# A second pair of spare-weight buffers in two expert stages, and another order in three of a kernel's product pairs

## The chip, the cores and the metric

The kernel runs on one core of one Trainium2 chip. The metric is device microseconds of one execution, as a median of several runs. All data is float32.

## What is computed

The reference is two networks one after the other, on 512 tokens of width 1024. The first has two layers. Each adds a mixer (pooling with chunked attention in layer 0, a Mamba-2 mixer in layer 1) and a hierarchical mixture of experts:

```python
g_val, g_idx = lax.top_k(g_prob, 1)                  # one of 4 groups
e_val, e_idx = lax.top_k(jax.nn.softmax(e_logits), 2) # two of its 8 experts
combine = jnp.sum(one_hot(expert_id, 32) * weights[..., None], axis=1)
hid = silu(einsum('td,edf->tef', t, w1)) * einsum('td,edf->tef', t, w3)   # f = 128
y = einsum('tef,efd->td', hid * combine[:, :, None], w2)
```

The second network has two layers too, on the 512 tokens and 256 tokens of context. Of the layer's wide input projection, `hx @ w_in`, come a bidirectional retention with per-head decay, a short convolution, a conformer convolution and a windowed attention; their four outputs are gated and merged, and `merged @ w_out` is added to the tokens:

```python
merged = sum(sigmoid(g) * (br @ w_branch[i]) for i, (g, br) in enumerate(zip(gates, (r, s, f, a))))
return merged @ w_out
```

In layer 0 the context is carried along; in layer 1 only its keys and values are needed.

## The kernel before, in words

Each engine has a program of its own, written out by hand in one order. `Count` (line 81) keeps the semaphore counts: a step of an engine is named (`pe.step`, `ve.step`), and another engine waits for the name (`pe.at`). What stands behind a waiting instruction on its engine waits too. Stages follow one another: mixer A, experts of layer 0, the Mamba-2 mixer, experts of layer 1, then the two layers of the second network.

**The expert stage** (`moe`, lines 789 to 900 on TensorE, 1335 on SyncE, 1557 on ScalarE, 2295 on VectorE, 2897 on POOL). A step handles two halves of 64 lanes, each with an expert of its own. There are 16 static steps for the 32 experts in order and 8 spare steps for experts that more than 64 tokens chose. `ORDER` (line 39) is two static steps, then a spare one, and so on: 24 steps. For step i TensorE does `rows_T` (transposes of the gathered token rows, two steps ahead), `up` (32 products 128x256, one step ahead), `hid_T` and `down` (8 products 128x512). `down` ends with the mark `step_done`.

Weights of a static expert, 1536 KB, are loaded by SyncE's queue into one of `HELD` = 7 buffers (line 370 ff.): five in `arena`, one in two ring slots and `square`, one in `hT`. Expert e waits for `step_done` of static step (e - HELD) // 2 (line 1338). Weights of spare experts come by indirect gathers from POOL (`spare`, line 2910): 128 rows of 12 KB per half into `spare_w`, two buffers in ring slots 0 to 5. Spare block j waits for the spare step before it. A block that no tokens need has row numbers out of bounds, and its gather moves no weights. POOL's queue holds, in this order: three row gathers (`fetch`), `spare(0)`, two more `fetch`, and then per step i one `fetch(i+5)`, which waits for the transposes of step i+2, the scatter of the output rows, which waits for VectorE's copy, and after a spare step the next `spare`. The work arrays of the router, `route_c` to `r4`, lie in `arena` between the row buffers and the static ones.

**Product pairs** (`pair`, line 671, on TensorE). Two blocks of 128 output columns of the second network, a and b, are computed together from half-sums of weights and of inputs, with seven products in place of eight (P1, P2, P6, P5, P7, P3 and one more); each is 4 x 2 instructions. VectorE makes the weight sums S1 to S4 (`w_sums`, line 1959, and `w_sum_4`), the input sums T1 to T4, and the sums of results C11, C22, C12 (`combine`, line 1981). ScalarE copies three partial results out of the banks (`copies`, line 1720): `copy_1` after P1, `copy_2` after P6, `copy_3` after P5 and C11. P6 waits for `copy_1`, S2 and T2; P7 for `copy_2`, S3 and T3; P3 for `copy_3` and S4; the last for C22 and T4. A pair takes 28 x 2 instructions.

Two places have no earlier pair to hide these steps. The first input pair follows the attention: VectorE does T1, T2, the weight sums, T4, T3, the gate multiplies of four chunks and a memset that marks `att_done` (lines 2666 to 2684). ScalarE does `ret_decay(0)`, which waits for `att_done`, `ret_strip(0)` and then `copies` (lines 1845 to 1847); these tables hold the powers of the decay and are first used in `ret_weights(0)`, after the second pair. The first output pair (`ready == "m"`) follows the merging: P1 waits for merged rows 0 to 3, P2 for rows 4 to 7 (lines 690 to 698).

## Time and profile before

| what | value |
|---|---|
| median of 3 runs | 3615.08 us (3606.56 to 3618.36) |
| the profiled execution's own time | 3612.57 us |
| its span, first to last instruction | 3610.8 us |
| TensorE busy | 3339.2 us (92%) |
| VectorE busy | 1730.4 us (48%) |
| ScalarE busy | 877.2 us (24%) |
| POOL busy | 128.5 us (4%) |
| mean granted TensorE clock | 0.967 of full |
| DMA | 393.88 MB, mean 109 GB/s |

Spans of the trace are read in microseconds from the first instruction. A granted clock of 1.00 is the upper of TensorE's two levels, 2.4 GHz, and 0.50 the lower, 1.2 GHz. "Idle before" is the time an engine stood before a group of instructions, and the arrow names what ended it. The expert stages lie at about 350 to 560 us and 1195 to 1400 us, the second network from about 1415 us on.

### The profile page before, as it was taken

What the parts mean: (1) busy time and instruction counts of PE and PEld (TensorE: products, weight loads), DVE (VectorE), ACT (ScalarE), POOL (GpSimd) and SP (SyncE); (2) the same over time, 40 slices, a digit from 0 to 9 for tenths busy, and PEclk for the clock granted to TensorE, in tenths of its full rate; (3) what the DMA queues carried; (4) which work ended last, traced back from release to release, by engine and by line L of the source; (5) the groups of instructions that cost most, each with busy time, mean ns of one, the idle gap of its engine ahead of it and who ended that gap; (6) DMA issues with size and microseconds to landing.
All of it is one profiled execution on the core that took longest, in us unless ns stands there. A gap on an engine that the chain in (4) does not pass through costs nothing.

```text
span 3610.8 us, 34772 instructions
## 1 busy us (share of the span) xinstructions
PE 3339.2 (92%) x12856; PEld 1965.0 (54%) x12856; DVE 1730.4 (48%) x3258; ACT 877.2 (24%) x1773; POOL 128.5 (4%) x132
## 2 busy tenths in 40 slices
PE   7987987999999797998899999999989889999998
PEld 3443553444444554555455555555544556778886
DVE  1153224555542324868533454444458853454554
ACT  2041222222331122025232121111121523222222
POOL 0000330000000230000000000000000000000000
PEclk9998998999999898999999999999999999999998
DMA  7625764767423783100111212222212011222331
GB/s 251 209 77 201 298 242 135 217 205 220 117 61 135 253 327 114 42 29 13 45 47 35 58 41 58 58 60 57 65 55 70 18 57 47 59 70 82 88 88 59
DMA packets 416917, 393.88 MB, mean 109 GB/s; under 512 B 27856, under 2 KB 353616, under 8 KB 409072
## 3 DMA queue, kind: packets, MB, share of 16 engines
q1 hardware_dynamic: 383200, 348.01, 30.8%
q10 hardware_dynamic: 15120, 23.68, 2.1%
q0 software_dynamic: 18432, 19.98, 1.7%
q8 instruction: 106, 1.74, 0.2%
q14 instruction: 59, 0.48, 0.0%
HBM read 440.78 MB, written 31.52 MB: 131 GB/s over the span
## 4 chain that ended last, share of the span: by engine, by line
PE 78%; DVE 7%; DMA 4%; ACT 4%; issue 2%; POOL 0%; ACTq 0%; DVEq 0%; POOLq 0%
PE psum L679 37%; PE psum L664 16%; PE psum L868 4%; PE psum L1059 3%; DVE arena L1944 2%; DMA ring<-in_moe_w,spare_u 2%; PE psum L1150 2%; PE psum L887 2%; ACT arena L1419 2%; PE psum L1198 2%; DMA ring<-in_w_branch 1%; PE psum L735 1%; PE psum L1218 1%; PE psum L1230 1%; PE psum L764 1%
## 5 line engine op out<-in xcount | busy, mean ns | idle before, releaser
L679 PE MATMUL psum<-arena,ring 128*128 128x384 f32 (+1 forms) x2592 | 750.6, 440 | 37.0 <-ACT part_sum L1419 23.4
L664 PE MATMUL psum<-hT,ring 128*128 128x512 f32 (+1 forms) x1728 | 706.0, 567 | 17.7 <-DVE hT L1937 15.4
L679 PEld LDWEIGHTS psum<-arena,ring 128*128 128x128 f32 x2592 | 494.3, 191 | 264.0 <-ACT part_sum L1419 25.8
L679 PE MATMUL psum<-hT,ring 128*128 128x384 f32 (+1 forms) x2176 | 621.8, 439 | 0.0
L664 PEld LDWEIGHTS psum<-hT,ring 128*128 128x128 f32 x1728 | 327.7, 192 | 390.0 <-issue 377.2
L679 PEld LDWEIGHTS psum<-hT,ring 128*128 128x128 f32 x2176 | 413.3, 190 | 188.7 <-issue 6.9
L1419 ACT ACTIVATE arena<-psum 128x512 f32<-128x512 f32 (+5 forms) x501 | 210.2, 466 | 571.3 <-PE psum L664 285.4
L1941 DVE TENSOR_TENSOR ring<-ring 128x512 f32<-128x512 f32 (+1 forms) x336 | 215.7, 661 | 269.9 <-PE psum L679 267.3
L1419 ACT ACTIVATE part_sum<-psum 128x384 f32<-128x384 f32 (+1 forms) x324 | 142.7, 440 | 817.7 <-PE psum L679 813.8
L1411 ACT ACTIVATE arena<-psum,cols 128x256 f32<-128x256 f32 (+3 forms) x280 | 133.1, 494 | 683.3 <-PE psum L868 227.7
L1941 DVE TENSOR_TENSOR psum<-psum,part_sum 128x384 f32<-128x384 f32 (+1 forms) x244 | 120.0, 497 | 288.8 <-PE psum L679 280.0
L1941 DVE TENSOR_TENSOR arena<-arena 128x512 f32<-128x512 f32 (+13 forms) x252 | 186.3, 753 | 107.4 <-ACT arena L1419 57.9
L1944 DVE SCALAR_TENSOR_TENSOR arena<-arena,psum 128x128 f32<-128x128 f32 (+3 forms) x284 | 115.2, 430 | 252.9 <-ACT arena L1411 225.3
L1944 DVE SCALAR_TENSOR_TENSOR arena<-arena,vec 128x783 f32<-128x783 f32 (+1 forms) x256 | 228.7, 893 | 9.1
L1411 ACT ACTIVATE arena<-arena,cols 128x512 f32<-128x512 f32 (+8 forms) x199 | 158.1, 828 | 63.5 <-DVE cols L2684 20.3
L868 PE MATMUL psum<-ring,arena 128*64 128x256 f32 x640 | 100.3, 429 | 27.2 <-DMA ring<-in_moe_w,spare_u 27.2
L1941 DVE TENSOR_TENSOR arena<-psum,part_sum 128x384 f32<-128x384 f32 (+1 forms) x80 | 40.8, 510 | 170.6 <-PE psum L679 170.4
L679 PE MATMUL psum<-arena,square 128*128 128x384 f32 (+1 forms) x384 | 113.9, 432 | 3.7 <-DVE arena L1941 3.7
L1059 PE MATMUL psum<-arena,ring 128*128 128x512 f32 x256 | 110.7, 593 | 0.0
L868 PE MATMUL psum<-arena 128*64 128x256 f32 x768 | 102.5, 383 | 0.0
L868 PEld LDWEIGHTS psum<-ring,arena 128*64 128x64 f32 x640 | 65.4, 155 | 63.2 <-DMA ring<-in_moe_w,spare_u 37.4
L1944 DVE SCALAR_TENSOR_TENSOR xT<-psum,cols,xT 128x512 f32<-128x512 f32 (+1 forms) x64 | 37.6, 611 | 125.7 <-PE psum L1059 65.1
(233 smaller groups left out, 2995.0 us busy)
## 6 DMA issues: line engine op xcount, KB each, us to landing
ring<-in_w_in SPq DMA_DIRECT2D x172, 512.0 KB, 4.1
arena<-in_moe_w SPq DMA_DIRECT2D x48, 1536.0 KB
ring<-in_ada_w SPq DMA_DIRECT2D x96, 512.0 KB, 5.5
ring<-in_ssm_w_in SPq DMA_DIRECT2D x48, 512.0 KB, 6.5
ring<-in_w_mod SPq DMA_DIRECT2D x48, 512.0 KB, 4.8
ring<-in_w_branch SPq DMA_DIRECT2D x64, 256.0 KB, 3.1
hT<-in_moe_w SPq DMA_DIRECT2D x8, 1536.0 KB
ring<-in_mix_w_in SPq DMA_DIRECT2D x16, 512.0 KB, 7.8
```

The source lines that it names most:

```text
L664: mm = nc.tensor.matmul(b[:, 0:n], ws[k // 8][0][:, k % 8, :], rhs(k)[:, o:o + n], start=(k == 0), stop=(k == nk - 1))
L679: mm = nc.tensor.matmul(flat(bank_, nb), lhs[:, k, :], rhs(k), start=(start and k == 0), stop=(k == kd_ - 1), skip_group_check=True)
L735: mm = nc.tensor.matmul(b[32 * j:32 * j + 32, :], csilu[:, int(q >= 6), k, :], w, start=(k == 0), stop=(k == KD - 1), skip_group_check=True)
L868: mm = nc.tensor.matmul(b[LANES * h:LANES * h + LANES, 0:2 * P], rowsT[:, i % 2, k, LANES * h:LANES * h + LANES], step_weights(s, h, 2 * P ...
L887: mm = nc.tensor.matmul(b[LANES * h:LANES * h + LANES, :], hidT[:, i % 2, LANES * h:LANES * h + LANES], step_weights(s, h, w0, S), start=T ...
L1059: mm = nc.tensor.matmul(b, ws[k // 8][0][:, k % 8, :], yT[:, k, :], start=(k == 0), stop=(k == 15))
L1150: mm = nc.tensor.matmul(b[:, 0:w], z_w[c][0][:, k, :], hT[:, k, o:o + w], start=(k == 0), stop=(k == KD - 1))
L1198: mm = nc.tensor.matmul(b[0:64, :], v_tok[:, t, 64 * j:64 * j + 64], pT2[:, kb, :], start=(i == 0), stop=(i == len(tiles) - 1))
L1411: return nc.scalar.activation(out_, in_, f, bias=bias, scale=scale, **kw)
L1419: return nc.scalar.activation(out_, in_, ACT.Copy)
L1941: return v.tensor_tensor(out_, in0, in1, op)
L1944: return v.scalar_tensor_tensor(out_, in0, s, in1, op0, op1)
```

## The change

The static experts get six buffers in place of seven, and the spare experts four in place of two: the new pair is the area of the router's work arrays and the freed static buffer. Spare block j then waits for the spare step two before it. Block 1's gather goes into the POOL queue behind `fetch(4)`, behind a wait for the last token transposes and for `w_slot`, and in layer 0 behind two memsets that clear the new buffers. `w_slot` gets a tile of its own. Experts 4 and 5 take the buffers, and the waits, that experts 5 and 6 had. In the first input pair of each layer, VectorE makes the weight sums ahead of the input sums and T3 ahead of T4, and ScalarE's `copies` and VectorE's `combine` of this pair go ahead of the decay tables. In the first output pair of each layer P5 goes between P1 and P2; `w_sums` waits for P6 too.

```diff
-HELD = 7
+HELD = 6
...
+        w_slot = sb("w_slot", [P, STEPS])[:, :]
...
-        held = [in_thirds(arena[:, held_at + EW * i:held_at + EW * (i + 1)]) for i in (3, 4, 0, 1, 2)]
+        held = [in_thirds(arena[:, held_at + EW * i:held_at + EW * (i + 1)]) for i in (3, 4, 0, 1)]
...
-        spare_w = [ring[:, 3 * i:3 * i + 3, :, :].rearrange("p a k n -> p (a k n)") for i in range(2)]
+        assert routed_at + EW <= held_at
+        spare_tiles = [ring[:, 0:3].rearrange("p a k n -> p (a k n)"), ring[:, 3:6].rearrange("p a k n -> p (a k n)"),
+                       arena[:, routed_at:routed_at + EW], arena[:, held_at + 2 * EW:held_at + 3 * EW]]
+        spare_w = [in_thirds(t) for t in spare_tiles]
...
                 product(x, wa[:, 0:kd_, :], low(0), True, ("P1", a))
-                w, w_full = job(*a, "0")
                 if ready == "m":
+                    z, z_full = job(*a, "1")
+                    eng.wait_ge(vector_done, pe.at(("S1", a)))
+                    eng.wait_ge(vector_done, pe.at(("T1", ready, a[1])))
+                    product(z, s(0), total(0), True, ("P5", a))
                     for c in range(4, 8):
                         eng.wait_ge(vector_done, pe.at(("mrg", a[1], c)))
+                w, w_full = job(*a, "0")
                 product(w, wa[:, kd_:2 * kd_, :], high(0), True, ("P2", a))
...
                 product(x, s(1), total(1), False, ("P6", a))
-                z, z_full = job(*a, "1")
-                eng.wait_ge(vector_done, pe.at(("S1", a)))
-                product(z, s(0), total(0), True, ("P5", a))
+                if ready != "m":
+                    z, z_full = job(*a, "1")
+                    eng.wait_ge(vector_done, pe.at(("S1", a)))
+                    product(z, s(0), total(0), True, ("P5", a))
...
-                            eng.wait_ge(spare_landed[h], pe.at(("spare", l, s - STATIC, h)))
+                            eng.wait_ge(spare_landed[2 * (s % 2) + h], pe.at(("spare", l, s - STATIC, h)))
...
-                    elif e == 5:
+                    elif e == 4:
                         eng.wait_ge(tensor_done, sp.at(("full",) + jobname("route", l)))
-                    elif e == 6:
+                    elif e == 5:
                         eng.wait_ge(tensor_done, sp.at(("full",) + jobname("h_tok", l, 3, 1)))
...
                     todo = pairs(l)
+                    copies(*todo[0])
                     ret_decay(0)
                     ret_strip(0)
-                    copies(*todo[0])
...
                 if last:
                     eng.wait_ge(tensor_done, ve.at(("P5", last)))
+                    eng.wait_ge(tensor_done, ve.at(("P6", last)))
...
+                    if l == 0:
+                        eng.wait_ge(tensor_done, ve.at(("full",) + jobname("att_z", l, 0, "x0")))
+                    w_sums(*todo[0])
+                    w_sum_4(*todo[0])
                     eng.wait_ge(tensor_done, ve.at(("full",) + jobname("pt2", l, 7, x_tiles(l)[-1], "x")))
...
                     tt(rows_of(1), hi1, rows_of(0), ALU.subtract).then_inc(vector_done, ve.step(("T2", "h", l)))
-                    if l == 0:
-                        eng.wait_ge(tensor_done, ve.at(("full",) + jobname("att_z", l, 0, "x0")))
-                    w_sums(*todo[0])
-                    w_sum_4(*todo[0])
+                    tt(lo1, hi1, lo1, ALU.subtract).then_inc(vector_done, ve.step(("T3", "h", l)))
                     eng.wait_ge(vector_done, ve.own())
                     tt(rows_of(2), hi0, rows_of(1), ALU.subtract).then_inc(vector_done, ve.step(("T4", "h", l)))
-                    tt(lo1, hi1, lo1, ALU.subtract).then_inc(vector_done, ve.step(("T3", "h", l)))
...
+                    combine(*todo[0])
                     decay(0)
-                    combine(*todo[0])
...
                 def spare(j):
 
-                    if j:
-                        eng.wait_ge(tensor_done, po.at(("step_done", l, STATIC + j - 1)))
+                    if j >= 2:
+                        eng.wait_ge(tensor_done, po.at(("step_done", l, STATIC + j - 2)))
+                    elif j:
+                        eng.wait_ge(tensor_done, po.at(("full",) + jobname("h_tok", l, 3, 1)))
+                        eng.wait_ge(vector_done, po.at(("w_slot", l)))
+                        if l == 0:
+                            g.memset(spare_tiles[2], 0.0).then_inc(gpsimd_done, po.step())
+                            g.memset(spare_tiles[3], 0.0).then_inc(gpsimd_done, po.step("spare_clear"))
+                            eng.wait_ge(gpsimd_done, po.at("spare_clear"))
...
                     for h in range(2):
-                        eng.indirect_dma_start(spare_w[h], None, a[f"moe_w_{l}"].rearrange("e p n -> (e p) n"),
+                        q = 2 * (j % 2) + h
+                        eng.indirect_dma_start(spare_tiles[q], None, a[f"moe_w_{l}"].rearrange("e p n -> (e p) n"),
...
                 fetch(DEEP)
                 fetch(DEEP + 1)
+                spare(1)
...
-                    if s >= STATIC and s + 1 < STEPS:
-                        spare(s + 1 - STATIC)
+                    if s >= STATIC and s + 2 < STEPS:
+                        spare(s + 2 - STATIC)
```

## Rows read from the trace of the kernel before

**Rows 1.** The page, costliest groups of instructions.

```profile
L1419 ACT ACTIVATE part_sum<-psum 128x384 f32<-128x384 f32 (+1 forms) x324 | 142.7, 440 | 817.7 <-PE psum L679 813.8
...
L868 PE MATMUL psum<-ring,arena 128*64 128x256 f32 x640 | 100.3, 429 | 27.2 <-DMA ring<-in_moe_w,spare_u 27.2
```

**Rows 2.** Chain of waits, layer 1's experts: start us, us, what.

```profile
1194.75 3.58 PE psum L843 x16
...
1212.77 3.45 PE psum L868 x32
...
1229.32 7.17 DMA ring<-in_moe_w,spare_u
1236.58 5.36 PE psum L868 x32
...
1361.09 3.45 PE psum L868 x32
```

**Rows 3.** Chain of waits, layer 0's experts.

```profile
372.83 3.45 PE psum L868 x32
...
518.82 3.45 PE psum L868 x32
...
525.27 3.45 PE psum L868 x32
```

**Rows 4.** Timeline of POOL: start, us, engine, line, what, idle before.

```profile
362.23 0.98 POOL L2906 DMA_INDIRECT arena<-h_dram,pair_u  x1 [0.61 <-PE psum L853]
371.23 0.98 POOL L2906 DMA_INDIRECT arena<-h_dram,pair_u  x1 [8.02 <-PE psum L853]
...
1227.99 1.02 POOL L2917 DMA_INDIRECT ring<-in_moe_w,spare_u  x1 [0.30 <-issue]
```

**Rows 5.** Windows: us, busy (count) of five engines, PEclk, DMA share, GB/s.

```profile
395.41:510.60 115.19, 104.08 (x735) 61.14 (x736) 30.28 (x60) 24.40 (x60) 39.65 (x40) 0.94 0.87 322
442.86:465.69 22.83, 19.58 (x148) 11.56 (x148) 6.06 (x12) 4.86 (x12) 9.04 (x9) 1.00 0.98 359
1213.00:1229.00 16.00, 16.00 (x128) 9.37 (x124) 4.55 (x9) 3.24 (x8) 6.03 (x6) 1.00 0.95 374
1281.90:1302.50 20.60, 19.58 (x147) 11.59 (x147) 6.07 (x13) 4.86 (x12) 8.03 (x8) 1.00 0.93 353
```

**Rows 6.** Timeline of layer 0's first input pair.

```profile
1730.50 1.75 DVE L1941 TENSOR_TENSOR arena<-hT 128x1536 f32<-128x1536 f32 x1
...
1732.82 5.43 PE L679 MATMUL psum<-hT,ring 128*128 128x384 f32 x16
...
1733.96 2.61 DVE L1941 TENSOR_TENSOR ring<-ring 128x512 f32<-128x512 f32 x4
...
1744.43 0.06 DVE L2684 MEMSET cols<- 128x1 f32 x1
1744.58 3.86 ACT L1411 ACTIVATE arena<-arena,cols 128x512 f32<-128x512 f32 x5 [10.88 <-DVE cols L2684]
...
1748.87 7.36 PE L679 MATMUL psum<-arena,ring 128*128 128x384 f32 x16 [10.62 <-ACT part_sum L1419]
1748.94 0.56 DVE L1941 TENSOR_TENSOR arena<-psum,part_sum 128x384 f32<-128x384 f32 x1 [0.18 <-ACT part_sum L1419]
```

**Rows 7.** Timeline of layer 1's first input pair.

```profile
2908.52 3.72 PE L679 MATMUL psum<-hT,ring 128*128 128x256 f32 x16
...
2918.72 0.06 DVE L2684 MEMSET cols<- 128x1 f32 x1
...
2923.06 5.65 PE L679 MATMUL psum<-arena,ring 128*128 128x256 f32 x16 [10.82 <-ACT part_sum L1419]
```

**Rows 8.** Timeline of the first output pair, layer 0 and layer 1.

```profile
2595.99 16.39 PE L679 MATMUL psum<-arena,ring 128*128 128x384 f32 x45 [5.23 <-DVE arena L1941]
...
3537.88 15.30 PE L679 MATMUL psum<-arena,ring 128*128 128x256 f32 x62 [3.98 <-DVE arena L1941]
```

**Rows 9.** Groups of instructions by line and shape, VectorE's memset.

```profile
L2767 DVE MEMSET arena<- 128x1570 f32 x2 | 2.7, 1367 | 0.6 <-issue 0.6
```

More of the change, by code:

```diff
@@ L244, in program @@
         expert_landed = [sems(f"expert_{i}") for i in range(HELD)]
-        spare_landed = [sems(f"spare_{i}") for i in range(2)]
+        spare_landed = [sems(f"spare_{i}") for i in range(4)]
         y_back_landed = [sems(f"y_back_{i}") for i in range(4)]
@@ L350, in program @@
         logitT = scan_one
+        routed_at = mE.at
         route_c = mE.take(ROUTE_W)
@@ L359, in program @@
         spare_t = mE.take(2, 2 * SPARE)
-        w_slot = mE.take(STEPS)
         e_col = mE.take(16)
@@ L383, in step_thirds @@
         def step_thirds(s, h):
-            return held[(2 * s + h) % HELD] if s < STATIC else in_thirds(spare_w[h])
+            return held[(2 * s + h) % HELD] if s < STATIC else spare_w[2 * (s % 2) + h]
         def step_weights(s, h, at, n):
@@ L1343, in moe @@
                         eng.wait_ge(tensor_done, sp.at(("full",) + jobname("out" + "AM"[l], 0, "x")))
+                    elif e == 4:
+                        eng.wait_ge(tensor_done, sp.at(("full",) + jobname("route", l)))
                     elif e == 5:
-                        eng.wait_ge(tensor_done, sp.at(("full",) + jobname("route", l)))
-                    elif e == 6:
                         eng.wait_ge(tensor_done, sp.at(("full",) + jobname("h_tok", l, 3, 1)))
@@ L1349, in moe @@
                     to = held[e % HELD]
-                    if e % HELD < 5:
-                        i = (3, 4, 0, 1, 2)[e % HELD]
+                    if e % HELD < 4:
+                        i = (3, 4, 0, 1)[e % HELD]
                         eng.dma_start(arena[:, held_at + EW * i:held_at + EW * (i + 1)], w).then_inc(expert_landed[e % HELD], sp.landing(f"expert_{e % HELD}", ("expert", l, e)))
-                    elif e % HELD == 5:
-                        eng.dma_start(ring[:, RING2:RING2 + 2].rearrange("p s k n -> p (s k n)"), w[:, 0:2 * D]).then_inc(expert_landed[5], sp.landing("expert_5", None))
-                        eng.dma_start(to[2], w[:, 2 * D:3 * D]).then_inc(expert_landed[5], sp.landing("expert_5", ("expert", l, e)))
+                    elif e % HELD == 4:
+                        eng.dma_start(ring[:, RING2:RING2 + 2].rearrange("p s k n -> p (s k n)"), w[:, 0:2 * D]).then_inc(expert_landed[4], sp.landing("expert_4", None))
+                        eng.dma_start(to[2], w[:, 2 * D:3 * D]).then_inc(expert_landed[4], sp.landing("expert_4", ("expert", l, e)))
                     else:
-                        eng.dma_start(hT[:, 0:6, 0:S], w.rearrange("p (k n) -> p k n", n=S)).then_inc(expert_landed[6], sp.landing("expert_6", ("expert", l, e)))
+                        eng.dma_start(hT[:, 0:6, 0:S], w.rearrange("p (k n) -> p k n", n=S)).then_inc(expert_landed[5], sp.landing("expert_5", ("expert", l, e)))
                 eng.wait_ge(tensor_done, sp.at(("step_done", l, ORDER[-1])))
@@ L2292, in route @@
                 b, free = full("w_slots", l)
-                ts(w_slot, b[:, 0:STEPS], 0.5).then_inc(vector_done, ve.step(free))
+                ts(w_slot, b[:, 0:STEPS], 0.5).then_inc(vector_done, ve.step([free, ("w_slot", l)]))
             def moe(l):
@@ L2916, in spare @@
                     for h in range(2):
-                        eng.indirect_dma_start(spare_w[h], None, a[f"moe_w_{l}"].rearrange("e p n -> (e p) n"),
+                        q = 2 * (j % 2) + h
+                        eng.indirect_dma_start(spare_tiles[q], None, a[f"moe_w_{l}"].rearrange("e p n -> (e p) n"),
                                                bass.IndirectOffsetOnAxis(ap=spare_u[:, 2 * j + h:2 * j + h + 1], axis=0),
                                                bounds_check=row_limit,
-                                               oob_is_err=False).then_inc(spare_landed[h], po.landing(f"spare_{h}", ("spare", l, j, h)))
+                                               oob_is_err=False).then_inc(spare_landed[q], po.landing(f"spare_{q}", ("spare", l, j, h)))
                 eng.wait_ge(h_rows_stored, 64 * (l + 1))
```

## The prediction, made before the changed kernel was run

> **What bounds the kernel now.** I read the page first. TensorE is busy for 92% of the span, so time can only come from stretches in which it stands still or runs slowly. The costliest groups show one such wait in the expert stage: the up products of the spare steps stood 27.2 us for the gather into `ring` [rows 1]. The chain of waits of the two expert stages says how it comes about. A step without a wait starts 6.45 us after the one before (518.82 to 525.27), but every third step (a spare one) hangs on down product, copy, scatter issue, gather issue and the gather's landing, 7.17 us after its issue began at 1229.32 [rows 2, 3]. The POOL timeline has the first of the two gathers leave at 1227.99, after the scatter of the same step, and its product is due one step later [rows 4]. After the stand the up product runs at the lower clock level: 5.36 us in place of 3.45 [rows 2]. The windows of the DMA engines come next, since the weights flow through the same stage: their share is 0.87 over five groups, up to 0.98 in one [rows 5]. Then I looked at the places of the other two edits: TensorE stands 10.62 us (layer 0) and 10.82 us (layer 1) in the first input pair, for the copy that ScalarE makes only behind the decay tables, which wait for the memset that closes VectorE's gate multiplies [rows 6, 7], and 5.23 and 3.98 us in the first output pair, for the merged rows [rows 8].
>
> **Spare buffers, what goes.** With two pairs of buffers, the gather of spare block j waits for spare step j-2 instead of j-1. It keeps its place on the POOL queue, so a gather leaves as late in its group as before, but its product is due four steps later (25.8 us) and not one (6.45 us). Against 7 us of landing that is ample. Between the starts of up products 2 and 22 lie 20 steps: 372.83 to 525.27 is 152.4 us in layer 0, 1212.77 to 1361.09 is 148.3 in layer 1; at 6.45 each they would take 129.0. Upper bound of the gain: 23.4 + 19.3 = 42.7 us. It has the slow products in it.
>
> **Spare buffers, what comes.** The price is one static buffer: six, not seven. Expert e then waits for static step (e-6)//2, so both experts of static step s are released by step s-3. For even s that is three steps (19.35 us) ahead of use, for odd s two (12.9 us); before, only the second expert of an odd step had so little, the first had more. What the queue must carry per group of three steps is 322 GB/s x 115.19 us / 5 = 7.42 MB [rows 5], of it 6.3 MB static weights. In 19.35 us that asks for 383 GB/s. The trace's fullest stretches: 374 GB/s at a share of 0.95 over 16 us, 353 at 0.93 over 20.6, 359 at 0.98 over a whole group. Divided by their shares that is 394, 380 and 366 GB/s, so a group needs 18.8 to 20.3 us of full queue: as much as TensorE takes. At 394 a pair of experts with its share of rows (3.7 MB) lands 9.4 us after release, 3.5 us before an odd step wants it; at 366 the lag grows by 1 us a group and uses this up after three or four of the 6.7 groups, then 1 us a group is lost. Bounds per layer: 0 and 4 us of standing, to which slow products may add 2. I take the middle, 2.5. Net: 42.7 - 5 = 37.7 us.
>
> By the Trainium skill (HBM Reference, Specifications) a core has effectively about 358 GB/s, while one streaming alone measures about 425. The stretch with 374 GB/s lies above the first figure, so I don't take it for a cap; by it a group would last 20.7 us, by the second 17.5 and nothing would be lost.
>
> **Clearing the new buffers** (layer 0 alone): two POOL memsets of 128x3072. The trace has no POOL memset of size; VectorE's nearest is 1367 ns for 1570 elements [rows 9], which scales to 2.7 us each. Below nothing it can't go, as it stands on POOL's own queue; above, I allow three times that, 16 us for both. POOL stood 8.02 us between fetch 4 and fetch 5 there [rows 4]. The two new gathers (1.3 us each with issue gap) and the scatter and fetch behind the memsets move by what exceeds this, at most 11 us. Fetch 5 left at 371.2 and is transposed after up product 4, near 389, of which 7 us are landing; spare block 1 is due at up product 5, by 392, 28 us after POOL was free. I cost the clears at nothing; they count only above 17 us. The new waits for the transposes and the slot weights are met by then: the product for the latter ended at 1198.3 in layer 1, before fetch 3 [rows 2]. The buffer numbers of experts 4 and 5 shift with their waits; they are used 40 us later: nothing.
>
> **First input pair, layer 0** [rows 6]. ScalarE's first copies no longer stand behind the tables (3.86 us of exponentials, after the memset at 1744.43). VectorE makes the weight sums first (2.61 us), then T1, T2 (1.76 each): from 1730.6, T2 is there at 1736.7, before P1 and P2 end at 1738.2 (1732.82 + 5.43). So the third product starts at 1738.2 and not at 1748.87. T3 is ready at 1738.4, T4 at 1740.2. The third copy needs C11, which VectorE makes after the four gate multiplies and the memset (1744.5 + 0.56), the copy ends at 1745.7 and its product is due at 1746.3. Gain: 10.6 us, and the two products after the stand take 5.43 instead of 7.36: 1.9. Together 12.6. The tables, which with their last steps fill the 4.4 us from 1744.43 to 1748.87, now lie beside pair 1, seven products or 18.8 us on TensorE; their first user follows that pair: nothing.
>
> **Layer 1** [rows 7]: products are 1.73 us, so C11 is the next late one. P6 starts at 2912.4 instead of 2923.06 (10.7) and P6, P5 lose their slowness (5.65 to 3.7: 2.0). P5 and P7 end at 2917.5, but VectorE's memset is at 2918.72, C11 at 2919.2, the copy (0.4) at 2919.7: a stand of 2.3 us, with perhaps 1 us of lower clock behind it. Net 9.5 (bounds 8.5 and 10.5). P5 now waits for nothing there.
>
> **First output pair** [rows 8]. P5 moves into the stand for the merged rows 4 to 7: its needs (S1, T1) are met 1.7 us into it. The stand shrinks by one product (2.7 and 1.7 us). But P5 also covered the copy between P6 and P7: 0.44 us on average [rows 1] and hand-overs, some 0.7 and 0.6 now bare. Net 2.0 + 1.1 = 3.1. The added wait of VectorE for P6 is met where P5 still comes last, and here P6 is two products earlier than P5 was.
>
> **Sum.** 37.7 + 12.6 + 9.5 + 3.1 = 62.9 us off the profiled execution's 3612.57 (span 3610.8, 1.8 around it) gives 3549.7. The median of the runs, 3615.08, is 2.5 above that execution, so 3552 for the median.
>
> **Rivals.**
> A, the forecast: 3552, between 3545 (no stand on static weights) and 3560. Chance 0.66.
> B, the static weights become the bound: the queue sustains only 353 GB/s, the raw rate of its 20.6 us row. A group lasts 21.0 us, 1.65 too long, 10.7 us in 6.5 groups, less 3 of slack: 8 per layer, and up to 7 more if each stand slows an up product by 1.9. Time 3563 to 3577, 3570 taken. For it: the share 0.98 at 359 GB/s. Against: 374 over 16 us. Chance 0.23. The skill's 358 GB/s would land here.
> C, the edit of the input pair gives its gain back: the tables, now in pair 1, hold ScalarE when pair 1 wants its first copy. Layer 1 has little room: they follow pair 0's sums there, from about 2922, and pair 1 wants its first copy from 2925.3. Were they not hidden at all, they would cost 4.4 us a layer and 1.9 of slow products: 12.6 us together, 3565. Chance 0.06.
> D, slower than before: odd static steps. Should a pair of experts take L from release to landing, because rows, scatters and gathers share its engines, the step stands L - 12.9 and runs 1.9 slow. The expert stages lose against before from L = 14.3 on; to eat the other 25 us too, L must pass 16.1. At 17.5 a group takes 25.9 us against 22.7: 45 us in 14 groups, less 25, gives 3635. The trace speaks against it: two pairs went through in 16 us together. Chance 0.03.
> E, the change doesn't remove the wait: the gathers would have to land 25 us after issue; or the clears take over 17 us, once, and spare block 1 waits for the excess: 3555 to 3570. Chance 0.02.
>
> **How the numbers follow.** The range runs from 3542 (both bounds of A and the 2.5 between median and profiled run) to 3578 (B, C). About one in ten lies outside; each side's ends come from the bounds above. A measurement here can tell about 0.3%, 11 us, from no change. Only D is slower, and only a mixture of B, C and E near 3604 would be the same: faster 0.96, same 0.02, slower 0.02.
>
> **What the changed profile would show.** Right: no idle before up products for a gather into the spare buffers; steps of 6.45 us for most of both expert stages, clock 1.0; DMA share above 0.95; third product of the first input pair at once behind the second in layer 0, and a stand of about 2 us for a copy in layer 1; 2.5 us in place of 5.23 before the second product of the first output pair. Wrong: TensorE idle ended by a load from `in_moe_w` into the static buffers (B, or D if over 3 us each), up products of 5.36 us in many steps, a new wait of pair 1 for ScalarE's copy (C), POOL memsets of over 8 us (E).

## The result, and the profile after

The changed kernel takes 3562.2 us (median, 3559.4 to 3563.9), the kernel before 3612.6 in the same comparison: a ratio of 0.986 with a 95% interval of 0.9841 to 0.9879, 1.4% faster. The profiled executions have spans of 3610.8 and 3557.5 us, 53.3 apart, where the forecast's sum took off 62.9. By the medians it is 50.4 us, since the profiled execution was the fastest of its four.

The page of the changed kernel, whose parts 1 and 5 answer to [rows 1]:

```profile
span 3557.5 us, 34884 instructions
...
PE 3329.7 (94%) x12856; PEld 1959.4 (55%) x12856; DVE 1729.6 (49%) x3258; ACT 877.3 (25%) x1773; POOL 134.3 (4%) x134
...
L1428 ACT ACTIVATE part_sum<-psum 128x384 f32<-128x384 f32 (+1 forms) x324 | 142.5, 440 | 819.9 <-PE psum L683 807.8
```

Lines have moved by 4 to 19 (L679 is now L683, L868 is L877, L1419 is L1428). The group of up products that stood 27.2 us for spare gathers has no such wait left. TensorE does the same 12856 products in 9.5 us less busy time, and its mean granted clock is 0.971 where it was 0.967. Of POOL's 5.8 us more, the two clears are 5.3.

The chain of waits over layer 0's experts in the changed kernel (start us, us, what) answers to [rows 3]:

```profile
374.56 3.45 PE psum L877 x32
...
406.83 0.40 issue
407.23 3.67 PE psum L877 x32
...
446.18 1.34 issue
447.51 3.67 PE psum L877 x32
...
467.09 2.11 issue
469.21 3.67 PE psum L877 x32
...
508.15 3.45 PE psum L877 x32
```

From up product 2 to up product 22 it is now 508.15 - 374.56 = 133.6 us, where [rows 3] have 152.4. At 6.45 a step it would be 129.0 (the shortest measured below is 129.06). What is left are stands ahead of up products 7, 13 and 16, which the chain puts under "issue": it names nothing that ended them. In the program these products wait for the loads of their static experts from SyncE's queue, whose landings the view does not show; that the loads are what they stand for is what the experiments on bytes and release below show. All three are odd static steps (s = 5, 9, 11), those whose two experts are released only two steps ahead. Up products 4, 10, 19 and 22 have their experts released as late and don't stand.

The same view of layer 1, for [rows 2]:

```profile
1194.46 3.45 PE psum L877 x32
...
1226.73 2.56 issue
1229.29 5.26 PE psum L877 x32
...
1289.23 0.37 issue
1289.60 3.67 PE psum L877 x32
...
1328.54 3.45 PE psum L877 x32
```

Here it is 134.1 us where it was 148.3, with a stand of 2.56 us ahead of up product 7 that is followed by a product at the lower clock, 5.26 us for 3.45, and one of 0.37 ahead of up product 16. Up product 7 is the second of the odd static steps to use a buffer again.

Windows of the changed kernel in layer 0's expert stage (columns as in [rows 5]):

```profile
393.93:407.23 13.30, 12.90 (x99) 7.25 (x95) 4.39 (x9) 3.24 (x8) 4.05 (x4) 1.00 0.98 359
...
393.00:396.00 3.00, 3.00 (x28) 1.71 (x26) 1.38 (x2) 0.00 (x0) 1.24 (x2) 1.00 0.71 199
...
402.00:405.00 3.00, 3.00 (x29) 2.02 (x27) 0.64 (x2) 0.97 (x3) 0.42 (x1) 1.00 1.07 418
...
374.56:501.69 127.13, 123.28 (x934) 72.41 (x931) 38.33 (x76) 31.07 (x76) 49.51 (x49) 1.00 0.96 367
...
381.02:400.38 19.36, 19.36 (x149) 11.25 (x147) 6.05 (x12) 4.86 (x12) 8.07 (x8) 1.00 0.96 374
420.35:439.72 19.37, 19.37 (x150) 11.34 (x147) 6.05 (x12) 4.96 (x12) 8.09 (x8) 1.00 1.01 390
```

The share over the stage has risen from 0.87 to 0.96. A whole group of three steps moves at 390 GB/s in one place. But at 393 to 396 us the queue holds too little, 199 GB/s, because the next pair of experts is released only at 393.9, when down product 3 ends. Up product 7 gets its weights at 407.23, 13.3 us later, where they are due after 12.9. In these 13.3 us the engines moved 359 GB/s, or 4.8 MB, where the forecast counted 3.7 MB for this pair and its rows: the pair after it is issued 6.5 us into them. SyncE's timeline has the issues:

```profile
394.20 0.33 SPq L1363 DMA_DIRECT2D ring<-in_moe_w  x1
...
395.05 0.56 SPq L1366 DMA_DIRECT2D hT<-in_moe_w  x1
400.42 0.81 SPq L1361 DMA_DIRECT2D arena<-in_moe_w  x2
```

At the other stands the time from the end of the releasing down product to the up product is 14.2 and 15.0 us (up products 13 and 16 of layer 0), 15.5 and 13.3 (7 and 16 of layer 1).

The start of POOL's program, for [rows 4]:

```profile
364.71 2.67 POOL L2928 MEMSET arena<- 128x3072 f32 x1
367.31 2.67 POOL L2929 MEMSET arena<- 128x3072 f32 x1
370.25 1.00 POOL L2935 DMA_INDIRECT arena<-in_moe_w,spare_u  x1 [0.27 <-POOL arena L2929]
...
372.97 0.98 POOL L2916 DMA_INDIRECT arena<-h_dram,pair_u  x1 [0.43 <-issue]
```

The clears and the two new gathers fill the 8.02 us in which POOL stood before. Fetch 5 leaves at 372.97, 1.7 us later than before, and by 1.7 us the whole stage starts later in this execution (up product 2 at 374.56, before at 372.83).

TensorE's timeline at the first input pairs, layer 0 and layer 1, for [rows 6, 7]:

```profile
1699.04 5.43 PE L683 MATMUL psum<-hT,ring 128*128 128x384 f32 x16
...
1704.30 5.32 PE L683 MATMUL psum<-arena,ring 128*128 128x384 f32 x16
...
2862.94 3.72 PE L683 MATMUL psum<-hT,ring 128*128 128x256 f32 x16
2866.80 3.69 PE L683 MATMUL psum<-arena,ring 128*128 128x256 f32 x16
2870.33 1.89 PE L683 MATMUL psum<-hT,ring 128*128 128x256 f32 x8
2874.17 3.63 PE L683 MATMUL psum<-hT,ring 128*128 128x256 f32 x8 [1.95 <-ACT part_sum L1428]
2877.59 1.99 PE L683 MATMUL psum<-arena,ring 128*128 128x256 f32 x8
```

Layer 0 has no stand at all. Layer 1 has one of 1.95 us for the copy behind C11, and then eight products that take 3.63 us where eight at the upper clock take 1.89.

The same view at the first output pairs, for [rows 8]:

```profile
2549.55 7.09 PE L683 MATMUL psum<-arena,ring 128*128 128x384 f32 x16 [2.80 <-DVE arena L1950]
...
2557.26 3.14 PE L683 MATMUL psum<-arena,ring 128*128 128x384 f32 x9 [0.63 <-ACT part_sum L1428]
...
3485.24 4.08 PE L683 MATMUL psum<-arena,ring 128*128 128x256 f32 x10 [2.36 <-DVE arena L1950]
```

The stands of 5.23 and 3.98 us are 2.80 and 2.36, and the copy between P6 and P7 lies bare for 0.63 us.

**Where the 53.3 us come from.** I follow the same instruction in both traces and note by how much it is earlier. Each part's gain is its length before less its length after. Four product pairs have a new order, one input and one output pair in each layer:

| part | before, us | after, us | gain | forecast |
|---|---|---|---|---|
| layer 0, up product 2 to 22 | 152.4 | 133.6 | 18.9 | 20.9 |
| layer 1, up product 2 to 22 | 148.3 | 134.1 | 14.2 | 16.8 |
| first two pairs, layer 0 (P1 to the end of the second) | 49.2 | 36.4 | 12.8 | 12.6 |
| first two pairs, layer 1 | 43.4 | 34.7 | 8.7 | 9.5 |
| output pair, layer 0 (P1's block to the first token update) | 25.2 | 23.7 | 1.5 | 2.0 |
| output pair, layer 1 | 18.3 | 17.4 | 0.9 | 1.1 |
| everything else | | | -3.7 | 0 |

The last row lies at places that no edit touches. Of the 1.7 us by which up product 2 of layer 0 starts later, 1.5 are there at 328 us, ahead of the first clear and gather of the change. Later there are places where the clock falls in one execution and not in the other: a window of the changed kernel around one pair in layer 1 shows it.

```profile
3191.00:3201.00 10.00, 7.88 (x30) 6.30 (x28) 7.43 (x20) 2.60 (x7) 0.00 (x0) 0.83 0.18 52
```

The kernel before has a granted clock of 1.00 in the stretch that answers to it (3245 to 3255), and 1.7 us of the lead go there.

### The profile page after: what moved, and what is told of

It reads as the page before. It is cut to its first block, busy times and chain, and to the rows that moved or that the text cites. A ratio compares the mean times of both kernels' runs of the same rounds, so it can differ in the third digit from the quotient of the medians.

```text
span 3557.5 us, 34884 instructions
## 1 busy us (share of the span) xinstructions
PE 3329.7 (94%) x12856; PEld 1959.4 (55%) x12856; DVE 1729.6 (49%) x3258; ACT 877.3 (25%) x1773; POOL 134.3 (4%) x134
## 4 chain that ended last, share of the span: by engine, by line
PE 81%; DVE 6%; ACT 4%; DMA 2%; issue 2%; ACTq 0%; POOL 0%; DVEq 0%; POOLq 0%
PE psum L683 37%; PE psum L668 17%; PE psum L877 5%; PE psum L1068 3%; PE psum L896 2%; DVE arena L1953 2%; PE psum L1159 2%; ACT arena L1428 2%; PE psum L1207 2%; PE psum L862 1%; DMA ring<-in_w_branch 1%; PE psum L744 1%; PE psum L1227 1%; PE psum L1239 1%; PE psum L773 1%
## 5 line engine op out<-in xcount | busy, mean ns | idle before, releaser
L683 PE MATMUL psum<-arena,ring 128*128 128x384 f32 (+1 forms) x2592 | 747.7, 439 | 12.9 <-DVE arena L1950 5.2
L683 PE MATMUL psum<-hT,ring 128*128 128x384 f32 (+1 forms) x2176 | 623.7, 440 | 2.0 <-ACT part_sum L1428 2.0
L683 PEld LDWEIGHTS psum<-arena,ring 128*128 128x128 f32 x2592 | 492.7, 191 | 238.8 <-DVE psum L1950 11.5
L683 PEld LDWEIGHTS psum<-hT,ring 128*128 128x128 f32 x2176 | 414.1, 190 | 191.5 <-issue 6.9
L1428 ACT ACTIVATE arena<-psum 128x512 f32<-128x512 f32 (+5 forms) x501 | 210.4, 466 | 573.7 <-PE psum L668 289.0
L1428 ACT ACTIVATE part_sum<-psum 128x384 f32<-128x384 f32 (+1 forms) x324 | 142.5, 440 | 819.9 <-PE psum L683 807.8
L1953 DVE SCALAR_TENSOR_TENSOR arena<-arena,psum 128x384 f32<-128x384 f32 (+3 forms) x236 | 98.4, 447 | 222.6 <-ACT arena L1420 180.5
L683 PE MATMUL psum<-arena,square 128*128 128x384 f32 (+1 forms) x384 | 115.0, 435 | 3.8 <-DVE arena L1950 3.8
L877 PE MATMUL psum<-arena 128*64 128x256 f32 x960 | 110.0, 383 | 1.3 <-issue 1.3
L877 PEld LDWEIGHTS psum<-arena 128*64 128x64 f32 x960 | 70.0, 139 | 48.0 <-issue 18.1
L2327 DVE COPY arena<-psum 128x512 f32<-128x512 f32 x96 | 66.4, 691 | 57.2 <-PE psum L896 52.0
```

The costliest lines, as they stand in the source:

```text
L683: mm = nc.tensor.matmul(flat(bank_, nb), lhs[:, k, :], rhs(k), start=(start and k == 0), stop=(k == kd_ - 1), skip_group_check=True)
L877: mm = nc.tensor.matmul(b[LANES * h:LANES * h + LANES, 0:2 * P], rowsT[:, i % 2, k, LANES * h:LANES * h + LANES], step_weights(s, h, 2 * P ...
L1428: return nc.scalar.activation(out_, in_, ACT.Copy)
L1953: return v.scalar_tensor_tensor(out_, in0, s, in1, op0, op1)
L2327: v.tensor_copy(y_rows[:, i % DEEP, n * S:(n + 1) * S], b).then_inc(vector_done, ve.step([free, ("y_rows", l, i)]))
```

## The experiments

Three questions: what each part of the change is worth alone; why odd static steps still stand; and whether the layer 1 input pair's remainder can be had. In the second, the theory was that the release of a buffer comes too late for a queue that is nearly full. Rivals were a queue that cannot carry the bytes at all, and small packets of the spare gathers that slow the loads.

**Parts alone.** First the spare buffers without the other product orders (the hunks of the input and output pairs undone):

> The changed kernel with both pair edits undone, so the spare buffers alone. Theory 1 (the parts are independent, and the trace's landmarks give each its size): the expert stages keep their 133.6 and 134.1 us between up products 2 and 22, the pairs go back to their stands of 10.6 and 10.8 us: about 22 us over the changed kernel, 3584, or 29 below the kernel before. By the sum of the prediction it would be 38 below (3575). Rival: the parts overlap (an earlier expert stage lets the pairs start at another clock level or with other weights in the ring), then this run lies more than 4 us from 3584.

Measured: 3579.1 us, ratio 0.9917 (0.99 to 0.9934). The stages take 132.9 and 135.3 us, with stands at the same odd steps. The median is 4.9 us from the expected 3584, by the letter the rival's side, but 31.6 under the kernel before of its own comparison, where 29 were expected, and the landmarks of the trace are those of the theory. The input pairs have their old stands, as its timeline of TensorE shows:

```profile
1698.36 5.43 PE L683 MATMUL psum<-hT,ring 128*128 128x384 f32 x16
1714.41 2.29 PE L683 MATMUL psum<-arena,ring 128*128 128x384 f32 x3 [10.62 <-ACT part_sum L1423]
```

Then the reverse, the kernel before with only the pairs' new orders:

> The kernel before with the pair edits alone (seven static buffers, one pair of spare buffers). Theory 1: 22 us below the kernel before (12.8 and 7.2 in the input pairs, 1.5 and 0.9 in the output pairs), 3590; the expert stages unchanged, 152 and 148 us between up products 2 and 22. Prediction's sum: 25 below. Rival: less than 15 below, because part of what the changed kernel shows there is a matter of when it arrives.

Measured: 3596.4 us, ratio 0.9956 (0.9938 to 0.9973), 14.3 us under the kernel before of the same comparison. In the trace the first two pairs take 36.4 us in layer 0 and 34.7 in layer 1, as in the changed kernel. The two parts are 31.6 and 14.3 us by medians, together 45.9 of about 50: they add, within what these intervals can tell. By the median the pairs gave less than the 24 us that the table above has for them, and less than the 15 that the rival named. Both expert stages are as before (150.3 and 148.1), but the stage of layer 0 starts at 381.4 us instead of 372.8 in the profiled execution, the slowest of the four. This is jitter ahead of every edit: TensorE stood 3.25 us for a load of modulation weights there and not 1.70, and ran more of the following products at the lower clock. With these 8.6 us added to the 13.0 between the two spans, the trace speaks for the theory. The medians alone don't settle it.

**Price of the static buffer.** Six static buffers as in the changed kernel, but one spare pair as before (spare block j waits for the spare step before it; no clears; old pair orders):

```diff
-            return held[(2 * s + h) % HELD] if s < STATIC else spare_w[2 * (s % 2) + h]
+            return held[(2 * s + h) % HELD] if s < STATIC else spare_w[h]
```

> The kernel before with six static buffers in place of seven and still one pair of spare buffers: the price of the buffer by itself, with the wait for the spare gathers in place. Theory 2 (the queue is what static weights wait for, and it is not full while the spare gathers hold the stage at 22 to 23 us a group): no stand on static weights, 3613 within 4. Rival (it is the late release that makes odd static steps wait, whatever the load): odd static steps stand here too, 2 us or more a layer, 3617 or more.

Measured: 3603.1 us, ratio 0.9981 (0.9963 to 1.0), lower than both expectations. Giving the buffer away cost nothing by itself; the stages were even shorter, 147.8 and 143.6 us, and the waits for spare gathers fell from 27.2 to 23.7 us. No stand for a static load is seen, but for one of 0.2 us. So the price of the buffer only shows once the spare gathers no longer hold the steps back. That the gathers landed a little earlier fits loads that are released later and leave the queue to them, but no run settles this.

**Which step stands.** The spare step goes between the two static steps of a group, so that odd static steps come last:

```diff
-ORDER = [s for j in range(SPARE) for s in (2 * j, 2 * j + 1, STATIC + j)]
+ORDER = [s for j in range(SPARE) for s in ((2 * j, STATIC + j, 2 * j + 1) if j else (0, 1, STATIC))]
```

> The changed kernel with the spare step of groups 1 to 7 in the middle of its group instead of at its end, so that the last step is a static one and the first released experts are wanted three steps later instead of two. Theory 2 (backlog of a full queue that grows over the stage): the stage gets one step more of slack, the stands of 4.6 and 5.1 us a layer shrink to under 1.5 each, about 3555. Rival (each pair of experts that has only 12.9 us from release to use stands, backlog or not): one such window remains in each group, so the stands stay at 4 to 5 us a layer, 3562.

Measured: 3559.1 us, ratio 0.9856 (0.9839 to 0.9873). Layer 1 has no stand and takes 129.06 us; layer 0 takes 132.9, with stands in other places. Its chain of waits:

```profile
442.02 2.54 issue
444.57 3.67 PE psum L877 x32
...
502.87 0.81 issue
503.68 3.67 PE psum L877 x32
```

The stands move with the order, and 5.7 of the 9.5 us that both stages lost go: a short distance from release to use is part of their cause. The median lies between the two expectations and can't be told from the changed kernel's.

It is not all of it. Both stands that are left are ahead of static steps 8 and 14. Of the five steps that have two steps from release to use in this order (6, 8, 10, 12, 14), these are the two whose experts go to the buffers made of `ring` with `square` and of `hT`. Of the late released steps in the changed kernel's order, up products 7 and 16 have their experts there, and both stand in every stage of the six traces with its static loads and order (the changed kernel, parts alone, no empty gathers, C11 first, sums back, outputs back). Only up product 13 of layer 0, whose experts go to `arena`, stands by more than 0.3 us besides. So which buffer is loaded counts too. No run gave these steps other buffers, and why their loads land later stays open.

**Small packets.** With these inputs the spare gathers after the first block have all their row numbers out of bounds and move no weights. Here they are not issued:

```diff
+                        if j:
+                            continue
```

> The changed kernel without the gathers of spare blocks 1 to 7, which are empty for this input (each is 2 x 128 rows out of bounds); the gather of block 0 stays. Leaves out the loading of weights for those blocks. Theory 2 (bytes fill the queue): the small packets are a minor part, the stands at odd static steps shrink by a third at most, 3558 to 3562. Rival (the small packets of empty gathers are what delays the static weights): the stands vanish, 129.5 us between up products 2 and 22 in each layer, 3553.

Measured: 3565.8 us, ratio 0.9872 (0.9854 to 0.989), stages of 131.8 and 135.2 with stands at up products 7, 13 and 16 of layer 0 and 7 and 16 of layer 1 as before. The median lies above both expectations, the stages together are 0.7 us shorter. The rival of the small packets falls.

**Bytes.** Static experts from the seventh on load only the first two thirds of their weights, and their down products use what the buffer held:

> The changed kernel with experts 6 to 31 loading only their first two thirds (w1 and w3); the down products use what w2 part the buffer held. Leaves out a third of the static bytes, with the same releases. Theory 2: no stands at static steps, 129.1 us between up products 2 and 22, 3552. Rival (time from release to landing has a fixed part that a 12.9 us window misses at times): stands of 2 us or more stay in each layer, above 3556.

Measured: 3553.2 us, ratio 0.9841 (0.9823 to 0.9858), and not one stand in either stage. Its window over layer 0's stage:

```profile
374.96:504.03 129.07, 129.07 (x982) 75.02 (x980) 40.31 (x81) 32.40 (x80) 50.51 (x50) 1.00 0.75 268
```

The stands are the static loads' in the queue. This doesn't yet tell too many bytes from too late a release.

**Release.** All bytes again, but earlier. A buffer's first two thirds hold the up weights, which are free when the up product ends, one step before `step_done`:

```diff
+                for s in range(3, STATIC):
+                    eng.wait_ge(tensor_done, sp.at(("full",) + jobname("up", l, ORDER.index(s - 3))))
+                    for h in range(2):
+                        load(2 * s + h, 0, 2 * D)
+                    eng.wait_ge(tensor_done, sp.at(("step_done", l, s - 3)))
+                    for h in range(2):
+                        load(2 * s + h, 2 * D, 3 * D)
```

> The changed kernel with each static expert loaded in two parts: the first two thirds as soon as the up product that used the buffer is done (one step and the length of a down product earlier than now), the last third at step_done as now. Same bytes. Theory 2: the queue never runs dry, so a group takes the queue's own 18.8 to 19.6 us, 0 to 2 us of stands a layer, 3553 to 3557. Rival a (the mean rate of the queue is at its cap already, 367 GB/s over the stage): stands stay at 4 to 5 us, 3562. Rival b (more and smaller transfers cost more than they give): over 3563.

Measured: 3554.3 us, ratio 0.9846 (0.9828 to 0.9863), with no stand in either stage. Its windows:

```profile
372.61:501.67 129.06, 129.06 (x982) 74.97 (x980) 40.28 (x81) 32.41 (x80) 50.48 (x50) 1.00 0.95 359
...
381.00:400.00 19.00, 19.00 (x147) 11.03 (x145) 6.05 (x12) 4.86 (x12) 7.71 (x9) 1.00 1.02 391
...
420.00:440.00 20.00, 20.00 (x157) 11.67 (x155) 6.05 (x12) 4.86 (x12) 8.08 (x8) 1.00 1.02 398
```

TensorE is busy for all of the 129.06 us. The queue carries 391 to 398 GB/s where it is kept full. The bytes and the buffers are the same as in the changed kernel, so its stands are not the limit of what the queue can carry: an earlier release takes them away, those of `ring`, `square` and `hT` too. The loads also come in smaller pieces here, and no run has the pieces without the earlier release. The median is 7.9 us under the changed kernel's, but the intervals of the two ratios overlap; the stands' going is read from the trace.

Does the earlier release help the kernel before as well? Seven static buffers, one spare pair, released in two pieces:

> The kernel before, with nothing but the split release of its seven static buffers; one pair of spare buffers stays. Theory (the stands of the kernel before are those of a gather that is issued only when its one buffer comes free, whatever the static experts' loads do): the waits for the spare gathers stay, up 2 to up 22 takes 148 to 153 us in both layers, 3612. Rival (the gathers are late because they share the queue with static loads released in a lump, so that an earlier and smoother release helps them): 140 us or less, 3590 or less. A third (loads released earlier stand ahead of the gathers in the queue and make them later): over 155 us, 3620.

Measured: 3611.3 us, ratio 0.9993 (0.9982 to 1.0004), stages of 146.2 and 150.1 us. Its waits of TensorE (us in total, times, longest):

```profile
PE psum L868 <- DMA ring<-in_moe_w,spare_u: 27.7, 10, 7.2
```

The wait is that of [rows 1], 27.2 us there. The stands of the kernel before don't go with an earlier release of the static buffers; with the second spare pair they do. In this kernel the split is worth nothing that can be told.

**Layer 1's input pair.** VectorE makes C11 ahead of the gate multiplies, through the `mid` of `combine`:

```diff
-                    combine(*todo[0])
+                    combine(*todo[0], mid=att_gates)
```

> The changed kernel with C11 of the first input pair ahead of VectorE's gate multiplies and the memset instead of behind them; the decay tables stay behind the memset. Theory 3 (in layer 1 the third product waits for copy_3, which waits for C11, which waits for the gate multiplies; stand 1.95 us and some 1.6 us of lower clock after it): layer 1's input pair gains 3 to 4 us, layer 0's nothing, 3558 to 3559. Rival (weight sums and C22, now behind the multiplies, take the place of C11 as what is late): the stand moves to the last product, gain under 1 us or a loss of up to 3.

Measured: 3557.9 us, ratio 0.9856 (0.9838 to 0.9874). Its timeline of TensorE:

```profile
2868.44 3.69 PE L683 MATMUL psum<-arena,ring 128*128 128x256 f32 x16 [0.16 <-DVE arena L1950]
2871.97 3.62 PE L683 MATMUL psum<-hT,ring 128*128 128x256 f32 x16
2877.70 1.99 PE L683 MATMUL psum<-arena,ring 128*128 128x256 f32 x8 [2.11 <-DVE psum L1950]
```

The stand for the copy is gone, but the pair's last product now waits 2.11 us for C22, which VectorE makes behind the gate multiplies and the next pair's weight sums: the stand moved as the rival had it, while the median is the theory's. What went is the slow group behind the stand: from the first product of this pair to the first of the next it takes 2879.53 - 2864.56 = 14.97 us, the changed kernel 2879.41 - 2862.94 = 16.47. That is 1.5 us, under half of the 3 to 4 expected; the other 2.8 of the median can't be told from jitter.

**The sums' place.** Of the input pair's edits, the weight sums and T3 go back to their old places, and only the copies and `combine` stay ahead of the tables:

> After, with the weight sums of the input pair back behind the first difference tiles and T4 ahead of T3; the copies and the combining step stay ahead of the decay tables. Theory (nearly all of the pair's gain is the copies' move; the four sums take 2.6 us of VectorE ahead of C11 in layer 1 and are hidden behind products in layer 0): layer 0's pair within 1 us of the changed kernel's 36.4, layer 1's 2 to 3 us longer than 34.7, 3565. Rival (the sums' place is half of the gain): both pairs 5 us longer or more, 3572. A third (no part): 3562.

Measured: 3561.2 us, ratio 0.985 (0.9835 to 0.9865). The pairs are as long as in the changed kernel (the first two of layer 0 36.4 us, the first of layer 1 16.49 for 16.47). The third expectation holds: with the copies and `combine` ahead of the tables, this half of the edit is worth nothing. I had said 2 to 3 us for layer 1 and had not seen that the 2.6 us of sums are on VectorE ahead of C11 in either order.

**The output pairs' order.** Back to that of the kernel before:

> After, with the order of the products in the two output pairs as in the kernel before. Theory (the part is worth what the trace of the changed kernel shows, 1.5 us in layer 0 and 0.9 in layer 1): the stands ahead of the third product are 5.2 and 4.0 again, 3564.6. Rival (the rest of the gain is made up elsewhere in the pair, and the reorder is worth nothing): 3562.

Measured: 3563.6 us, ratio 0.9859 (0.9843 to 0.9874), 1.4 us over the changed kernel, too little to be told. The trace has the stands back:

```profile
2553.59 21.71 PE L683 MATMUL psum<-arena,ring 128*128 128x384 f32 x60 [5.23 <-DVE arena L1945]
...
3489.03 8.18 PE L683 MATMUL psum<-arena,ring 128*128 128x256 f32 x29 [3.98 <-DVE arena L1945]
```

The pairs take 25.6 and 18.3 us, 2.0 and 0.9 more than in the changed kernel, against 1.5 and 0.9 by the kernel before. The part is worth 2.4 to 2.9 us.

**Both improvements together**, the split release and C11 first:

> After, with the first two thirds of each static expert's buffer released at the end of its up product (as e7_split_release) and with the input pair's combining step ahead of the gate multiplies (as e8_c11_first). e7 measured 3554.3 and both its expert stages at 129.06 us; e8's trace shows layer 1's input pair 1.5 us shorter (14.97 us from the first product to the fifth instead of 16.47, and no product at the low clock), though its median was 4.3 under the changed kernel's. Theory (the two parts add, and the second is worth what its trace shows): 3552.8, stages 129.1 and 129.1, the input pair 15.0. Rival (the second part is worth its whole 4.3): 3550. A third (the 1.5 us is given back at the next place where the clock drops): 3554.

Measured: 3548.4 us (3544.4 to 3551.7), ratio 0.9817 (0.9803 to 0.983), stages of 129.07 us each and the pair at 14.98. It is the fastest of all and below all three expectations, some 0.4% ahead of the changed kernel by the two ratios. The kernel before measured 3615.5 in this comparison and 3611.9 in that of the two parts, so the ratios are the ones to compare. They put it 0.3% under the split release alone, more than the 1.5 us its trace explains, and their intervals just touch; the rest stays open.

## Why the prediction was right, and where it was off

The direction holds, and the wait that goes is the one forecast. The time, 3562.2, lies in the range of 3542 to 3578, but 10 us above the forecast's 3552 and outside the bounds that it gave its own case A (3545 to 3560). It is the width added for rivals B and C that covers it, though neither gives the reason. Its own sign of being wrong, TensorE idle for loads into the static buffers, is also seen in part. By its own steps:

- **Spare buffers, what goes.** Right. No up product waits for a spare gather, and without stands a stage takes 129.06 us, where the forecast's limit was 129.0. The upper bound of 42.7 us stands.
- **Spare buffers, what comes.** That odd static steps, two steps from release to use, stand is seen, but the term "Bounds per layer: 0 and 4 us of standing, to which slow products may add 2. I take the middle, 2.5" was mis-sized. The changed kernel loses 4.5 and 5.0 us against 129.06, slow products included. Four other traces with the same loads (parts alone, C11 first, sums back, outputs back) lose between 3.9 and 7.3. Over all ten stages the mean is 5.4. Six of the ten lie below the upper end of 6 (4 and 2 of slow products), four beyond it. The working failed in one place: it set a full queue's time for a group (18.8 to 20.3 us) against TensorE's, let a pair land 9.4 us after its release, and had the 3.5 us of slack used up by a lag that grows over three or four groups. The queue isn't full just around an odd step's release (199 GB/s at 393 to 396 us), and later the next pair's load shares the engines. Where TensorE stood, the weights came 13.3 to 15.5 us after their release and not 9.4, against 12.9 until they are due. Nor does a lag grow: up product 7, in the third group, is the first to stand, in layer 1 it has the longest stand, and the last two odd steps of each stage have none. The working also took all buffers alike, where most stands are at two of them. Rival B, the queue's rate, had 8 us a layer and more, so the stands lie between it and the forecast; its reason falls, since with the same bytes released earlier nothing stands. Rival D's 14.3 us and more from release to landing were met at two of the stands, but not at every odd step, as D had it.
- **The skill's figure.** The Trainium skill (HBM Reference, Specifications) has about 358 GB/s as a core's effective share and 425 for one streaming alone. The split release's windows show 391 and 398 GB/s over 19 and 20 us, above the first and below the second. It was right not to use the first as a cap on one core at work.
- **Clearing.** Right, and nearer than such scaling deserves: 2.67 us each, forecast 2.7, hidden in POOL's stand of 8.02. That the rate of another engine fitted was luck.
- **Input pairs.** Layer 0: 12.8 for 12.6. Layer 1: 8.7 for 9.5; the stand was smaller than forecast (1.95 for 2.3), while the slow products behind it cost 1.8 and not "perhaps 1". Of the edits credited with it, the move of the copies and `combine` does the work; the two were not parted. Rival C, that pair 1 would now want ScalarE, is not seen.
- **Output pairs.** 2.4 for 3.1. The stand shrank by 2.43 and 1.62 us (forecast 2.7 and 1.7) and the copy's bare time is as forecast, 0.63 and 0.52.
- **Between the parts.** The forecast had nothing there. 3.7 us net are lost in the profiled pair of executions, at places no edit touches; e2's start of layer 0's experts, 8.6 us late, shows that single executions differ by as much.

So of the 9.6 us between 62.9 and 53.3, 4.6 are stands in the expert stages, 0.5 the input pairs' balance, 0.7 the output pairs and 3.7 jitter.

## What to carry to other kernels

A buffer moved from a stream that has slack to one that waits can be nearly free, but count for every use the time from release to need, not only bytes per group over bandwidth: in this kernel a queue whose mean was under what it can carry still starved steps whose loads were released late. When such a stand is left, look for a part of the buffer that is free earlier; releasing the up weights ahead of the down weights took the stands away with no byte less. Look, too, at which buffer's steps stand, and not only at how far ahead they are released. And before crediting an edit of several moves, undo them one by one: here half of one was worth nothing.

## What the runs showed of the hardware

- One core's DMA engines carried 391 to 398 GB/s over 19 to 20 us with the weight loads of the split release, and 390 over 19.4 us with those of the changed kernel (1536 KB an expert), with row gathers, scatters and out-of-bounds gathers mixed in.
- Two static experts needed 13.3 to 15.5 us from release to use at the five stands of the changed kernel. Four of the five are ahead of products whose weights lie in `ring`, `square` and `hT`.
- Leaving out the out-of-bounds gathers changed nothing that can be told (133.6 and 134.1 us a stage with them, 131.8 and 135.2 without), though in the kernel before a product stood for one that landed 7.17 us after its issue began.
- POOL's memset of 128x3072 float32 took 2.67 us.
- A stand of 1.95 us was followed by eight products at nearly half speed (3.63 us for 1.89), and one of 2.56 by a product of 5.26 for 3.45, but stands of 1.34 and 2.11 in layer 0's experts only by 3.67. What decides this was not tried.
